# 73 wide down tiles instead of 30, 34 down tiles split by GpSimd instead of 24, gathers and last activations moved

## What is computed

```python
def _peer(x, wq, sub_keys, down, up):
    qry = (t @ wq).reshape(T, PEER_HEADS, 2, PEER_DKEY // 2)
    s = jnp.einsum('thcd,hcnd->thcn', qry, sub_keys)
    s1, i1 = lax.top_k(s[:, :, 0], PEER_TOPK)          # 16 of 128, twice
    s2, i2 = lax.top_k(s[:, :, 1], PEER_TOPK)
    cand_s = s1[..., :, None] + s2[..., None, :]       # 256 candidates
    top_s, top_pos = lax.top_k(cand_s, PEER_TOPK)
    expert = ...                                       # i1 * 128 + i2 of the 16 best
    gate = jax.nn.softmax(top_s, axis=-1)
    a = jax.nn.gelu(jnp.einsum('ted,td->te', down[eb], tb), approximate=False)
    return jnp.einsum('te,ted->td', a * gb, up[eb])    # 128 experts of 16384 a token
```

## Time and profile before

| | |
|---|---|
| runs | 1058.26, 1061.05, 1066.93 us, median 1061.05 |
| profiled execution | 1059.69 us, its span 1057.9 us, mean granted clock 0.992 |
| TensorE (PE) busy | 1028.5 us, 97% |
| VectorE (DVE) busy | 797.0 us, 75% |
| ScalarE (ACT) busy | 535.8 us, 51% |
| GpSimd (POOL) busy | 103.4 us, 10% |
| read from HBM | 200.60 MB, 191 GB/s over the span |

### The profile page before, as it was taken

How to read it: one execution, slowest core, us unless ns; L and a number is a source line. 1 busy time by engine, 2 the same in 40 slices (tenths; PEclk the granted TensorE clock), 3 DMA queues, 4 the chain that set the end, 5 groups by cost and what they waited for, 6 DMA issues and landing times.

```text
span 1057.9 us, 18483 instructions
## 1 busy us (share of the span) xinstructions
PE 1028.5 (97%) x7388; PEld 912.5 (86%) x7388; DVE 797.0 (75%) x1434; ACT 535.8 (51%) x870; POOL 103.4 (10%) x86
## 2 busy tenths in 40 slices
PE   8999999999999789999999999999999999999996
PEld 8988888898799789979999999988888888888885
DVE  5667767857599987567989988798889885555575
ACT  5564544554465436566555555444444445545551
POOL 3000000000079400112221000000000000000000
PEclk9999999999999989999999999999999999999999
DMA  9943334733346536788888555655555556656671
GB/s 319 384 143 100 101 121 159 248 128 102 116 156 196 178 120 197 243 301 292 300 282 291 172 177 182 208 186 178 173 169 178 167 172 197 188 193 198 189 249 40
DMA packets 56373, 203.44 MB, mean 192 GB/s; under 512 B 6480, under 2 KB 6528, under 8 KB 55904
## 3 DMA queue, kind: packets, MB, share of 16 engines
q1 hardware_dynamic: 49824, 178.80, 51.9%
q0 software_dynamic: 6464, 23.46, 6.3%
HBM read 200.60 MB, written 1.11 MB: 191 GB/s over the span
## 4 chain that ended last, share of the span: by engine, by line
PE 85%; DVE 9%; DMA 3%; ACT 1%; issue 1%; SPq 0%; DVEq 0%
PE psS L1890 16%; PE psT L1890 16%; PE psG L1502 12%; PE psG L1503 11%; PE psG L1504 11%; PE psG L1835 4%; DMA raw<-in_down 2%; PE psG L1837 2%; PE psO L1858 1%; PE psO L1859 1%; DVE unit_c L1150 1%; DMA raw<-in_w_stream 1%; PE psT L1876 1%; PE psO L1782 1%; PE psS L1504 1%; PE psS L1502 1%
## 5 line engine op out<-in xcount | busy, mean ns | idle before, releaser
L730 ACT ACTIVATE hi<-raw 128x1024 fp32r<-128x1024 f32 x325 | 343.5, 1059 | 293.3 <-DMA raw<-in_up 180.4
L975 DVE TENSOR_TENSOR lo<-raw,hi 128x1024 fp32r<-128x1024 f32 x301 | 366.5, 1221 | 93.7 <-ACT hi L730 92.7
L1502 PE MATMUL psG<-b_two,hi 128*128 128x240 f32 (+1 forms) x848 | 238.4, 281 | 12.2 <-DVE lo L975 10.4
L1504 PE MATMUL psG<-b_two,lo 128*128 128x240 f32 (+1 forms) x848 | 234.5, 277 | 0.0
L1503 PE MATMUL psG<-b_two,hi 128*128 128x240 f32 (+1 forms) x848 | 234.5, 276 | 0.0
L1502 PEld LDWEIGHTS psG<-b_two,hi 128*128 128x128 f32 x848 | 161.3, 190 | 14.7 <-DVE lo L975 10.6
L1503 PEld LDWEIGHTS psG<-b_two,hi 128*128 128x128 f32 x848 | 161.4, 190 | 0.1
L1504 PEld LDWEIGHTS psG<-b_two,lo 128*128 128x128 f32 x848 | 161.2, 190 | 0.0
L1480 DVE TENSOR_TENSOR act_lo<-H,act_hi 128x256 fp32r<-128x256 f32 x128 | 53.7, 423 | 89.4 <-ACT act_hi L954 89.4
L1835 PE MATMUL psG<-b_two,hi 128*128 128x480 f32 x240 | 80.4, 386 | 2.6 <-DVE H L1425 2.6
L1890 PE MATMUL psS<-hi,act_hi 128*128 128x512 f32 x240 | 77.0, 402 | 0.0
(11 more groups left out here) (370 smaller groups left out, 1817.7 us busy)
## 6 DMA issues: line engine op xcount, KB each, us to landing
raw<-in_down SPq DMA_DIRECT2D x128, 512.0 KB, 3.6
raw<-in_up SPq DMA_DIRECT2D x128, 512.0 KB, 3.5
raw<-in_w_stream SPq DMA_DIRECT2D x73, 512.0 KB, 3.6
x_all<-apart_x POOLq DMA_DIRECT2D x16, 512.0 KB
w<-in_w SPq DMA_DIRECT2D x4, 512.0 KB, 13.4
xT<-in_xT SPq DMA_DIRECT2D x4, 256.0 KB, 4.7
raw<-in_w_stream SPq DMA_DIRECT2D x4, 256.0 KB, 5.6
memT<-in_memT SPq DMA_DIRECT2D x1, 1024.0 KB, 7.0
```

The lines of the kernel that those rows point to most:

```text
L730: act.activation(hi[hi_slot(n)][:], raw[slot(n)][:], ACT.Copy).then_inc(hi_done, 1)
L975: dve.tensor_tensor(lo[slot(n)][:], raw[slot(n)][:], hi[hi_slot(n)][:].bitcast(FP32), ALU.subtract)\
L1502: pe.matmul(out, hi_l, hi_r, start=start, stop=False)
L1504: return pe.matmul(out, lo_l, hi_r, start=False, stop=stop)
```

## The change

It makes six edits.

1. `POOL_TO` goes from 24 to 34 down tiles.
2. `WIDE` becomes tiles 48 to 120 without a gap, 73 tiles.
3. `APART_AT` goes from 50 + 3k to 52 + 3k, `APART_END` from 98 to 100; GpSimd asks for rows 6 tiles (was 5) and for the token 5 tiles (was 3) ahead of it.
4. The last four `act` stand in front of the split of the last up tile, and not behind it.
5. The first weight tile is requested by ScalarE in quarters and not by SyncE in halves, and split in quarters.
6. `one_hot` waits for `gates_done` of its own group number in one more case.

```diff
-POOL_FROM, POOL_TO = N1, N1 + 24
+POOL_FROM, POOL_TO = N1, N1 + 34
-WIDE = [j for j in range(48, 121) if j < HALF or j > 98 and j % 3]
+WIDE = range(48, 121)
-APART_AT = [50 + 3 * k for k in range(APART)]
-APART_END = 98
+APART_AT = [52 + 3 * k for k in range(APART)]
+APART_END = 100
...
-        if j + 4 < E_TILES:
+        if j + 4 < E_TILES - 4:
             out.append(("act", j + 4))
+        if j == E_TILES - LAST:
+            out += [("act", E_TILES - 4 + i) for i in range(4)] + [("late", E_TILES - 1)]
...
             for i in range(4):
                 part = slice(2 * i, 2 * i + 2)
                 sp.dma_start(xT[:, part, :], a["xT"][:, part, :]).then_inc(x_in[i], 16)
-                if i % 2 == 0:
-                    half = slice(i * D // 4, (i + 2) * D // 4)
-                    sp.dma_start(raw[0][:, half], a["w_stream"][0][:, half]).then_inc(first_in[i // 2], 16)
...
-                pool.wait_ge(tile_used, DOWN + APART_AT[k] - 5)
+                pool.wait_ge(tile_used, DOWN + APART_AT[k] - 6)
...
-                pool.wait_ge(tile_used, DOWN + APART_AT[k] - 3)
+                pool.wait_ge(tile_used, DOWN + APART_AT[k] - 5)
...
             for i in range(4):
-                part = slice(2 * i, 2 * i + 2)
+                quarter = slice(i * D // 4, (i + 1) * D // 4)
+                act.dma_start(raw[0][:, quarter], a["w_stream"][0][:, quarter]).then_inc(first_in[i], 16)
+            for i in range(4):
+                part, quarter = slice(2 * i, 2 * i + 2), slice(i * D // 4, (i + 1) * D // 4)
                 act.wait_ge(x_in[i], 16)
                 act.activation(o_hi[:, part, :], xT[:, part, :], ACT.Copy).then_inc(split_hi, 1)
...
+                act.wait_ge(first_in[i], 16)
+                act.activation(hi[0][:, quarter], raw[0][:, quarter], ACT.Copy).then_inc(hi_done if i == 3 else first_hi, 1)
...
-                elif what == "last" and j == E_TILES - LAST:
-                    split(UP + E_TILES - 1)
+                elif what == "late":
+                    split(UP + j)
...
-                if g == GROUPS:
+                if g == GROUPS or g % GROUPS > APART_GROUP and g % 2 == 0:
                     dve.wait_ge(gates_done, g)
```

More of the change, by code:

```diff
@@ L556, in build @@
         x_in = [sem(f"x_in{i}") for i in range(4)]
-        first_in = [sem(f"first_in{i}") for i in range(2 * FIRST)]
+        first_in = [sem(f"first_in{i}") for i in range(4 + 2)]
         warm_ready = sem("warm_ready")
@@ L640, in _ @@
                     half = slice(c * D // 2, (c + 1) * D // 2)
-                    sp.dma_start(raw[n][:, half], a["w_stream"][n][:, half]).then_inc(first_in[2 * n + c], 16)
+                    sp.dma_start(raw[n][:, half], a["w_stream"][n][:, half]).then_inc(first_in[4 + c], 16)
             for n in range(FIRST, ALL):
@@ L833, in _ @@
                     half = slice(c * D // 2, (c + 1) * D // 2)
-                    act.wait_ge(first_in[2 * n + c], 16)
+                    act.wait_ge(first_in[4 + c], 16)
                     act.activation(hi[n][:, half], raw[n][:, half], ACT.Copy).then_inc((first_hi, hi_done)[c], 1)
@@ L1114, in _ @@
                     .then_inc(split_lo, 1)
[L1115 to L1119, removed]
+                quarter = slice(i * D // 4, (i + 1) * D // 4)
+                dve.wait_ge(hi_done if i == 3 else first_hi, 1 if i == 3 else i + 1)
+                dve.tensor_tensor(lo[0][:, quarter], raw[0][:, quarter], hi[0][:, quarter].bitcast(FP32), ALU.subtract)\
+                    .then_inc(lo_done if i == 3 else first_lo, 1)
             for n in range(1, FIRST):
@@ L1122, in _ @@
                     half = slice(c * D // 2, (c + 1) * D // 2)
-                    dve.wait_ge((first_hi, hi_done)[c], n + 1)
+                    dve.wait_ge((first_hi, hi_done)[c], (4, 2)[c])
                     dve.tensor_tensor(lo[n][:, half], raw[n][:, half], hi[n][:, half].bitcast(FP32), ALU.subtract)\
@@ L1457, in _ @@
                             rest(UP + late)
-                elif what == "last" and j == E_TILES - LAST:
-                    rest(UP + E_TILES - 1)
+                elif what == "late":
+                    rest(UP + j)
                 elif what == "decode":
@@ L1545, in gemm @@
                             pe.wait_ge(turn_lo, turned_in - 1 + k // 4)
-                        if n < FIRST and k % 4 == 0:
-                            pe.wait_ge((first_lo, lo_done)[k // 4], n + 1)
+                        if n == 0 and k % 2 == 0:
+                            pe.wait_ge(lo_done if k == 6 else first_lo, 1 if k == 6 else k // 2 + 1)
+                        if n == 1 and k % 4 == 0:
+                            pe.wait_ge((first_lo, lo_done)[k // 4], (4, 2)[k // 4])
                         if n == 0 and k % 2 == 0:
```

5 lines of the change are left out of this document (removed).

## The result

The changed kernel took 1072.31 us (median of 5 runs, 1071.9 to 1073.6) against 1061.05 before: a ratio of 1.0104, 95% interval 1.0082 to 1.0127. It is slower by 11 us, where I had forecast no change (1060.8, range 1050 to 1072). Its profiled execution has a span of 1070.1 us.

The account below looks back on a forecast made before the run. TensorE, with work in 97% of the span, was taken to set the pace in places, DMA in tiles 46 to 64, TensorE and VectorE nearly level in 65 to 98. -5.9 + 7.5 - 0.6 + 0 - 1.0 - 0.3 = -0.3: 1060.8 us, range 1050 to 1072.

Parts of the forecast that it names:

- GpSimd's 34 splits: GpSimd also splits tiles 24 to 33: -13.2 us, plus 4.6 stall and 2.7 clock, net -5.9 us.
- The stall: At tile 34 TensorE waits 4.6 us for VectorE's split, as GpSimd's splits hold the decode steps ahead of it.
- Rival A: Decoding isn't held by GpSimd, so stall and cold clock (7.3 us) vanish: 1053.5 us; chance 0.14 alone.
- 43 wide tiles: VectorE becomes the bound in tiles 65 to 98, +7.5 us; tiles 99 to 120 give -0.6.
- B: VectorE's lateness in tiles 65 to 98 is absorbed: +1.3 us instead of +7.5, 1054.6 us; chance 0.14 alone.
- The -0.6 of tiles 99 to 120: Eight more wide tiles there: VectorE's added work is hidden, TensorE saves 0.075 us each.
- Gathers: New places and earlier requests cost 0 us (-3 to +2), as no VectorE wait for a gather is seen.
- "I keep half" of the waits for landings: Tiles 65 to 98: half of VectorE's 8.4 us of waits for late weight tiles stays, 4.2 us.
- rival C: The landing loop sets tiles 65 to 98 once landings stay above about 5 us: +19.9 us, 1073.2; chance 0.16.
- Tiles 46 to 64: DMA sets the pace in this stretch of 54.90 us, 2.87 us a tile at 305 GB/s.
- Last activations -1.0: Making the last four ahead of the last up tile's split removes TensorE's 1.0 us wait.
- Start -0.3: First weight tile in quarters from ScalarE's queue, commands leaving SyncE: -0.3 us (0 to -1.5).

Follow-up runs that it names:

- e1: The changed kernel with the 30 wide tiles of before, all other edits kept; 1061.77 us, ratio 1.0004.
- f3: The changed kernel with the 30 wide tiles, gathers and products of before; 1056.41 us, ratio 0.9944.
- j1: The changed kernel, 73 wide tiles and new product places kept, rows and tokens requested 5 and 3 tiles ahead as before; 1063.79 us, ratio 1.0020.
- f4: f3 with the decode steps behind tiles 28 to 42 instead of 22 to 36; 1046.05 us, ratio 0.9862.
- e2: The kernel before with the 73 wide tiles as its only edit; 1068.76 us, ratio 1.0068.
- i1: The changed kernel with 30 wide tiles, new product places, rows and tokens requested 5 and 3 tiles ahead as before; 1057.16 us, ratio 0.9947.
- h2: f4 with 73 wide tiles instead of 30; 1056.81 us, ratio 0.9960.
- i2: The changed kernel with 30 wide tiles and old product places, rows and tokens requested 6 and 5 tiles ahead; 1061.14 us, ratio 1.0006.
- h1: h2 with VectorE splitting tile j+2 instead of j+3 in its place for tile j, from tile 46 to 121; 1048.94 us, ratio 0.9893.
- h4: f4 (30 wide tiles) with VectorE splitting tile j+2 instead of j+3, from tile 46 to 121; 1043.54 us, ratio 0.9837.
- f1: The changed kernel with 30 wide tiles and products one tile later, at 53 + 3k; 1060.87 us, ratio 1.0006.
- e4: The changed kernel with only the first 3 of 16 token broadcasts made (outputs of 16 tokens wrong); 1063.34 us, ratio 1.0019.

## Why the prediction was wrong, point by point

- **GpSimd's 34 splits: right, in mechanism and size.** Forecast -5.9; tiles 24 to 34 gave -6.1. The stall was forecast at 4.6 us with a ready time of 395.2; TensorE waited 4.6, and `lo` was there at 395.03. To the tenth that is luck: with the same splits e1, f3 and j1 waited 5.3 to 5.9 us. f4 shows that the `decode` steps ahead of the split make the stall. The hold by turns is in VectorE's timeline, which answers to the earlier trace rows, beside GpSimd's:

```profile
376.69 3.31 DVE L1348 TENSOR_TENSOR picked_e<-iota,picked_f 128x2048 f16<-128x2048 f16 x1
380.04 3.31 DVE L1354 TENSOR_TENSOR picked_e<-picked_e,ranked_f 128x2048 f16<-128x2048 f16 x1
...
387.18 1.22 DVE L1348 TENSOR_TENSOR picked_e<-iota,picked_f 128x2048 f16<-128x2048 f16 x1
388.43 1.23 DVE L1354 TENSOR_TENSOR picked_e<-picked_e,ranked_f 128x2048 f16<-128x2048 f16 x1
...
393.81 2.35 DVE L974 TENSOR_TENSOR lo<-raw,hi 128x1024 fp32r<-128x1024 f32 x2
...
373.46 12.14 POOL L696 TENSOR_TENSOR lo<-raw,hi 128x1024 fp32r<-128x1024 f32 x4 [0.22 <-ACT hi L729]
```

  The same instruction takes 3.31 us while GpSimd splits and 1.22 after its last split. Rival A fell. The Trainium skill (SBUF — State Buffer, Who interferes with whom) states that such a pair exclude each other, and this trace agrees (3.31 against 1.22). GpSimd pays too: its four last splits take 12.14 us, 3.04 each against 2.41.
- **43 wide tiles: right in size in two of four measurements.** Forecast 7.5 - 0.6 = 6.9. From before to e2 it is 0.68 points, 7.2 us; from i1 to j1, 0.73 points, 7.7 us. But beside the new gathers (e1 to the changed kernel) it is 1.00 points, 10.6 us, and from f4 to h2 0.98. VectorE's work in tiles 65 to 98 was forecast at 105.8 and was 106.7. B fell. The -0.6 of tiles 99 to 120 failed: it is +1.2, and TensorE waits there (64.48 busy of 66.05). Two things go with it: the kernels with few wide tiles take 66.0 with the gathers' end at 100 (e1, i1) and 64.6 to 64.7 with 98 (i2, f3), and e2, wide with 98, takes 65.6.
- **Gathers: the step that failed.** It was priced at 0, from -3 to +2, with the reason that no VectorE wait for a gather is seen. Their new lead costs 6.0 to 6.6 us beside 30 wide tiles and 8.9 beside 73. The reason looked at who waits for the gathers, and not at who waits for the weight tiles that land beside them: VectorE for the copies (14.3 us, with the old lead 6.4), and TensorE behind it for `add_low` and for the gates' `one_hot`, a wait that no term of the sum had. I had written down that "a different third of the landings is late", and did not ask in front of which slot that third then stands.
- **"I keep half" of the waits for landings: failed with it.** Waits of 4.2 us were kept; with the old lead they are 6.4 (j1), with the new 14.3. This is the way of rival C, which came out nearly to the number: 3.53 us a tile in 65 to 98 (3.6 forecast), 1072.3 in all (1073.2). Its 3.6 was a pick between two paces and not worked out, so the closeness is partly luck. Its signs were both there, VectorE idle for over 8 us and a stretch over 118. What it had wrong is its condition. Landings need not stay above 5 us: here one in three took 5.8 on the mean, the others 4.0 to 4.5. And the loop isn't fixed: h1, which against h2 only changes what stands behind a landing, has VectorE idle for 0.9 us.
- **Tiles 46 to 64: the bound was misread.** I had called DMA the pace at 2.87 a tile (305 GB/s). h4, which differs from f4 in VectorE's order alone, runs them in 52.5 at 319 GB/s where f4 takes 55.0, so some 2.5 us of the 54.9 were order.
- **Last activations -1.0: right.** From up tile 119 to the end it is 29.3 against 30.4 us, and the wait for `act_lo` is gone; ScalarE made the last activations beside others at 1042.95, ahead of the last tile's copy.
- **Start -0.3: not told from scatter.** Tile 23 ends 0.34 us sooner than before. But with the new start it ends at 362.9 to 366.1 in the other kernels, and with the old one at 363.7 and 364.5 (e2). Two commands leave SyncE, and not four as the prediction has it first. `one_hot`'s new wait did nothing that is seen.
- **The chances didn't fit the range.** With 0.2 below 1050.4 and 0.2 above 1071.7, some 0.4 lie outside 1050 to 1072, and not 0.2. The time fell 0.3 us above that range; that it is so near is no merit of the forecast, whose own range ended at 1067.

Along one path (before, f3, i1, j1, changed) the ratios give each part a price, with some 3 us of uncertainty on each. From before to f3 (splits, activations, start) it is -5.9 us (-7.2 forecast), the places of the products +0.3, the wide tiles +7.7 and the lead +8.9, in all +11.0. Steps between ratios have to sum to the whole, so this is no check; over e1 instead of j1 the lead costs 6.0 and the wide tiles 10.6. The two cost more together than apart.

## What to carry to other kernels

Of a transfer that is moved, ask which other transfers now land beside it and what stands behind each of those in the engines' lists. "Nobody waits for it" prices only its own lateness. Where two engines are nearly level, put the instruction that frees the next engine's buffer ahead of the one that waits for a landing: here that was worth 8 us by medians with the same work (10 in the profiled stretch), while the 43 wide tiles could save TensorE some 3 us (43 x 0.075). And when work goes to GpSimd, price the VectorE work that runs beside it by turns, and move what can wait behind GpSimd's last piece.

## What the runs showed of the hardware

- By its semaphore a 0.5 MB weight tile lands 3.6 to 3.8 us after its request on the mean where only weights are on their way (tiles 99 to 120), 4.2 (e2) to 5.0 (f1) beside the gathers in tiles 65 to 98, and after 7.15 in the single case above.
- In the changed kernel waits of TensorE of only 1.9, 2.0 and 2.2 us were each followed by some 3.4 us at half clock, which costs 1.7 more, so the clock can nearly double the loss by a wait. It is not so behind every such wait: f3 kept full clock behind one of 1.95 us, e4 behind one of 2.28. In tiles 65 to 98 of j1 the longest wait was 1.6 us, and it lost none.
- VectorE's fp16 and GpSimd's f32 tensor_tensor work, both with two inputs in SBUF, take turns: 1.22 us became 3.31 and 2.41 became 3.04.
